# The first block's down projection by pairs of weight panels, seven block products for eight, on one Trainium2 core

## What is computed

```python
h = jnp.square(jax.nn.relu(jnp.einsum("bsd,df->bsf", x, w_ff1[l])))
ff = jnp.einsum("bsf,fd->bsd", h, w_ff2[l])
x = layer_norm(DEEPNORM_ALPHA * x + ff, ln2_g[l], ln2_b[l])
```

## Time and profile before

| | us |
|---|---|
| median of the runs (1448.5 to 1450.94) | 1448.59 |
| profiled execution: span from first to last instruction | 1446.2 |
| what lies around the span, by the median | 2.4 |
| feed-forward part of the first block (64 panels), matmuls | 348.4 |
| TensorE busy | 1419.5 |
| VectorE busy | 820.0 |
| ScalarE busy | 612.0 |
| GpSimd busy | 134.1 |

### The profile page before, as it was taken

How to read it: one execution, slowest core, us unless ns; L and a number is a source line. 1 busy time by engine, 2 the same in 40 slices (tenths; PEclk the granted TensorE clock), 3 DMA queues, 4 the chain that set the end, 5 groups by cost and what they waited for, 6 DMA issues and landing times.

```text
span 1446.2 us, 20161 instructions
## 1 busy us (share of the span) xinstructions
PE 1419.5 (98%) x7966; PEld 1137.2 (79%) x7966; DVE 820.0 (57%) x1408; ACT 612.0 (42%) x1113; POOL 134.1 (9%) x119
## 2 busy tenths in 40 slices
PE   8999999999999999999999999999999999999998
PEld 6777677788878888888877777786778888888887
DVE  4645555557574343443468776676565763664464
ACT  4644455543363242322336755345444431442334
POOL 0000000002200000000012010350020110110012
PEclk9999999999999999999999999999999999999999
DMA  7222221113223222222223212110232322223212
GB/s 254 73 83 92 80 89 64 68 58 117 102 62 114 96 93 103 93 103 96 93 100 133 95 65 74 59 47 1 96 109 73 116 102 96 94 102 102 84 66 70
DMA packets 41501, 130.94 MB, mean 91 GB/s; under 512 B 4928, under 2 KB 7360, under 8 KB 41408
## 3 DMA queue, kind: packets, MB, share of 16 engines
q1 hardware_dynamic: 40544, 128.60, 25.4%
q10 hardware_dynamic: 864, 1.05, 0.2%
HBM read 124.92 MB, written 4.19 MB: 89 GB/s over the span
## 4 chain that ended last, share of the span: by engine, by line
PE 88%; DVE 5%; ACT 3%; issue 2%; DMA 1%; POOL 0%; SPq 0%; POOLq 0%; DVEq 0%; ACTq 0%
PE bank L1300 85%; PE bank L1303 3%; ACT Fm L1697 2%; DVE Fm L2160 1%; DVE Wlo L2055 1%; DVE Fm L2055 1%; ACT Whi L1697 1%; DVE Fm L2063 1%; DMA Fm<-in_relb_dram 1%; SPq L2756 0%; POOL Fm L2659 0%; DVE Xf L2055 0%; DMA Fm<-in_x_dram 0%; DVE sm L2059 0%; DVE Fm L2059 0%
## 5 line engine op out<-in xcount | busy, mean ns | idle before, releaser
L1300 PE MATMUL bank<-Rm,Whi 128*128 128x512 f32 (+1 forms) x2840 | 874.8, 389 | 9.2 <-ACT Whi L1697 6.0
L1300 PEld LDWEIGHTS bank<-Rm,Whi 128*128 128x128 f32 x2840 | 533.0, 188 | 119.9 <-ACT Whi L1697 6.0
L1300 PE MATMUL bank<-Rm,Wlo 128*128 128x512 f32 (+1 forms) x1420 | 565.6, 398 | 1.1 <-issue 0.9
L2055 DVE TENSOR_TENSOR Wlo<-Wraw,Whi 128x1024 fp32r<-128x1024 f32 (+2 forms) x225 | 284.2, 1267 | 141.6 <-ACT Whi L1697 141.0
L1300 PEld LDWEIGHTS bank<-Rm,Wlo 128*128 128x128 f32 x1420 | 267.7, 189 | 61.7 <-issue 7.6
L1697 ACT ACTIVATE Whi<-Wraw 128x1024 fp32r<-128x1024 f32 (+2 forms) x225 | 232.5, 1038 | 191.8 <-PE bank L1300 186.2
L1300 PE MATMUL bank<-Xr,Whi 128*128 128x512 f32 (+1 forms) x760 | 228.5, 382 | 0.0
L2659 POOL TENSOR_TENSOR Fm<-Fm 128x512 f32<-128x512 f32 (+1 forms) x89 | 112.3, 1269 | 773.5 <-ACT Fm L1697 480.3
L1300 PEld LDWEIGHTS bank<-Xr,Whi 128*128 128x128 f32 x760 | 141.1, 188 | 27.9
L1697 ACT ACTIVATE Fm<-bank 128x512 f32<-128x512 f32 (+4 forms) x200 | 92.3, 482 | 147.8 <-PE bank L1300 103.2
L2055 DVE TENSOR_TENSOR Fm<-Fm,bank 128x512 f32<-128x512 f32 (+2 forms) x130 | 77.8, 622 | 120.7 <-PE bank L1300 120.2
(11 more groups left out here) (100 smaller groups left out, 712.7 us busy)
## 6 DMA issues: line engine op xcount, KB each, us to landing
Wraw<-in_w_in_dram SPq DMA_DIRECT2D x67, 512.0 KB, 3.2
Wraw<-in_w_ff_dram SPq DMA_DIRECT2D x64, 512.0 KB, 3.2
Wraw<-in_w_up_dram SPq DMA_DIRECT2D x44, 512.0 KB, 3.2
Wraw<-in_w_o_dram SPq DMA_DIRECT2D x16, 512.0 KB, 3.2
Wraw<-in_w_down_dram SPq DMA_DIRECT2D x16, 512.0 KB, 3.1
Wraw<-in_w_ab_dram SPq DMA_DIRECT2D x8, 512.0 KB, 3.2
Wraw<-in_w_down_end_dram SPq DMA_DIRECT2D x8, 384.0 KB, 2.8
Fm<-in_relb_dram SPq DMA_DIRECT2D x8, 256.0 KB, 4.1
```

The costliest lines, as they stand in the source:

```text
L1300: return e.matmul(o, l, r, start=first, stop=last)
L2055: return e.tensor_tensor(o, x, y, op)
```

## The change

Down panels are taken in pairs (two output tiles, n and n+1). Over the 8 hidden tiles of a group, the pair is a product of 2 x 2 blocks: the two output tiles and the two halves of the contraction (4 row tiles each) on the weight side, and tokens 0 to 255 (`EARLIER`) and 256 to 511 (`LATER`) on the other. It is now made by seven products of blocks instead of eight, after Winograd: each product is 4 steps of three matmuls of 256 columns. The order of rows in `w_ff2` is changed on the host so that the halves are even and odd hidden tiles.

- Weights: of a pair's four half panels a11, a12, a21, a22 GpSimd makes s1 = a21 + a22, s2 = s1 - a11, s4 = a12 - s2, s3 = a11 - a21 (128 x 512 each) from the raw panels. They are split in two *parts* of 1024 elements (s1 and s2; s4 and s3) by ScalarE (`blocksplit`) and VectorE (`blocklow`). Of the second panel only the half a22 is split as before; the first is split whole. The buffers of the sums and of their parts are single.
- Hidden tiles: after each second up panel, `hidden` makes three sums on GpSimd (one of 512 elements, two of 256) and the high and low parts of 256 + 3 x 512 elements in place of 2 x 512.
- Outputs: the products land in three banks (`total`, `single`, `fifth`), and VectorE adds them to the output tiles in six `fold`s: 256 elements four times, 512 twice. Product 6 is added on product 1 in its bank, 3 on 5, 7 on 6; so product 6 waits for fold 1, 3 for fold 5, 7 for fold 6.
- ALPHA is multiplied in by ScalarE after up panels 0 to 7 of the first group.
- The P ring has 6 banks. Loads wait for the sums of the pair 4 panels before, too, and the constants' load for the last hidden tiles.
- In the last group both `sum` items come after the pair.

```diff
+PRODUCTS = (1, 2, 5, 6, 4, 3, 7)
...
         while st["splits"] < min(len(PANELS), upto) and st["splits"] - HL < st["done"]:
...
+            n = st["splits"]
+            do("split", n)
             st["splits"] += 1
+            if pair_of(n) == n - 1:
+                do("blocks", n - 1)
+                st["sums"] += 1
...
+    def sum_parts(upto):
+        while st["parts"] < upto and st["parts"] // 2 < st["sums"]:
+            do("blocksplit", PAIRS[st["parts"] // 2], st["parts"] % 2)
+            do("blocklow", PAIRS[st["parts"] // 2], st["parts"] % 2)
+            st["parts"] += 1
...
             if p == LOW_AT:
                 low_weights()
+                sum_parts(2 * st["pairs"] + 2)
...
+    def seven_products(name, i):
+
+        n = take(name, i)
+        take(name, i + 1)
+        r = st["pairs"]
+        for bank in ("total", "single", "fifth"):
+            do(bank, n)
+        sum_parts(2 * r + 1)
+        do("product", n, 1)
+        sum_parts(2 * r + 2)
+        low_weights(st["taken"] + 1)
+        do("fold", n, 1)
+        do("product", n, 2)
+        low_weights()
+        do("product", n, 5)
+        do("fold", n, 5)
+        do("product", n, 6)
+        do("fold", n, 6)
+        sum_parts(2 * r + 3)
+        do("product", n, 4)
+        do("fold", n, 4)
+        do("product", n, 3)
+        do("fold", n, 3)
+        do("product", n, 7)
+        do("fold", n, 7)
+        st["pairs"] += 1
+        st["done"] = n + 2
...
+    do("ring", "P", (3, 7, 1, 2, 4, 0))
     for kind, i in FF1:
         if kind == "up":
             n = first[i] if i < 3 else project("w_ff1", i)
             do("relu2", i)
+            if i % 2:
+                do("hidden", i // 2)
+            if i < 8:
+                do("alpha", i)
         else:
-            for m in range(8):
-                n = project("w_ff2", 8 * i + m)
-                do("down", n)
+            for m in range(0, 8, 2):
+                seven_products("w_ff2", 8 * i + m)
                 if i == 3:
                     do("sum", 1, m)
+                    do("sum", 1, m + 1)
...
+                elif what == "product":
+                    n, p = i
...
+                    if p in (1, 2, 5):
+                        bank_free({1: "total", 2: "single", 5: "fifth"}[p], n)
+                    else:
+                        if p != 4:
+                            w.wait_ge(SG["fold"], fold_end(n, {6: 1, 3: 5, 7: 6}[p]))
...
+                    for k in range(4):
+                        q = 4 * g + k
+                        w.wait_ge(SG["hid_hi"], moving_made(q, p))
+                        w.wait_ge(SG["hid_lo"], moving_made(q, p))
+                        xh, xl = moving(q, p)
+                        s = slice(128 * k, 128 * k + 128)
+                        add(o, lo[:, s], xh, p in (1, 2, 5) and k == 0)
+                        add(o, hi[:, s], xl)
+                        m = add(o, hi[:, s], xh, False, k == 3)
+                    m.then_inc(SG["product"], 1)
...
+                elif what == "blocksplit":
+                    n, half_ = i
+                    r = PAIR_NO[n]
+                    w.wait_ge(SG["blocks"], 4 * r + 2 * half_ + 2)
+                    if r > 0:
+                        w.wait_ge(SG["product"], product_end(PAIRS[r - 1], 7 if half_ else 6))
+                    hi, _, raw = combined(half_)
+                    act(hi, raw).then_inc(SG["block_hi"], 1)
...
+                elif what == "hidden":
+                    q, = i
+                    f, b = F(SQUARE + 2 * q % 4), F(SQUARE + 2 * q % 4 + 1)
+                    for n, of in ((3, f[:, EARLIER]), (0, b), (1, F(SUMS)), (2, F(SUMS + 1))):
+                        if n in (0, 3):
+                            w.wait_ge(SG["squared"], 2 * q + (1 if n == 3 else 2))
+                        else:
+                            w.wait_ge(SG["hid_sums"], 3 * q + (1 if n == 1 else 3))
...
+                        act(hidden_part(q, n)[0], of).then_inc(SG["hid_hi"], 1)
...
+                elif what == "blocks":
...
+                    w.wait_ge(*loaded(n))
+                    w.wait_ge(*loaded(n + 1))
+                    if r > 0:
+                        w.wait_ge(SG["block_lo"], 2 * r - 1)
+                    tt(s1, a21, a22, ALU.add).then_inc(SG["blocks"], 1)
+                    w.wait_ge(SG["blocks"], 4 * r + 1)
+                    tt(s2, s1, a11, ALU.subtract).then_inc(SG["blocks"], 1)
+                    w.wait_ge(SG["blocks"], 4 * r + 2)
+                    if r > 0:
+                        w.wait_ge(SG["block_lo"], 2 * r)
+                    tt(s4, a12, s2, ALU.subtract).then_inc(SG["blocks"], 1)
+                    tt(s3, a11, a21, ALU.subtract).then_inc(SG["blocks"], 1)
...
                     if n >= RAW:
                         w.wait_ge(SG["w_hi"], n - RAW + 1)
                         w.wait_ge(*low_part(n - RAW))
+                        if pair_of(n - RAW) is not None:
+                            w.wait_ge(SG["blocks"], 4 * PAIR_NO[pair_of(n - RAW)] + 4)
```

More of the change, by code:

```diff
@@ L119, with pair_of, product_end @@
 NTH = {p: n for n, p in enumerate(PANELS)}
+DOUBLE = ("w_ff2",)
+PAIRS = [n for n, (name, i) in enumerate(PANELS) if name in DOUBLE and i % 2 == 0]
+PAIR_NO = {n: r for r, n in enumerate(PAIRS)}
+def pair_of(n):
+    name, i = PANELS[n]
+    return n - i % 2 if name in DOUBLE else None
+PRODUCTS = (1, 2, 5, 6, 4, 3, 7)
+def product_end(n, p):
+    return 7 * PAIR_NO[n] + PRODUCTS.index(p) + 1
 RAW = 4
@@ L145, in order_of_work @@
     work, side, later = [], [], []
-    st = {"loads": 0, "splits": 0, "lows": 0, "taken": 0, "done": 0}
+    st = {"loads": 0, "splits": 0, "lows": 0, "taken": 0, "done": 0, "sums": 0, "parts": 0, "pairs": 0}
     def do(*item):
@@ L907, in sb @@
             return ctx.enter_context(nc.sbuf_tensor(name, shape, dt))
+        with nc.sbuf_tensor("Er", [128, 49, 512], F32R) as Er:
+            pass
         Fm = sb("Fm", [128, 49, 512])
@@ L1078, in low_part, with finished @@
             return SG["w_lo"], at("low", n)
+        def finished(n):
+            if pair_of(n) is not None:
+                return SG["product"], product_end(pair_of(n), 2 if pair_of(n) == n else 4)
+            return SG["panel"], n + 1 - sum(2 for m in PAIRS if m < n)
         def emptied(n):
@@ L1236, in summed @@
             if tag == 1:
-                return SG["down"], at("down", NTH["w_ff2", 24 + j])
+                return SG["fold"], fold_end(NTH["w_ff2", 24 + j - j % 2], 7 if j % 2 else 3)
             if tag == 2:
@@ L1300, in mm, with add @@
                 return e.matmul(o, l, r, start=first, stop=last)
+            def add(o, l, r, first=False, last=False):
+                return e.matmul(o, l, r, start=first, stop=last, skip_group_check=True)
             def tr(o, x):
@@ L1699, in panel @@
             def panel(n):
-                w.wait_ge(SG["panel"], n + 1)
+                w.wait_ge(*finished(n))
                 return bank("panel", n)
@@ new lines, in vector_engine @@
+                    tt(F(SQUARE + j % 4), F(RELU + j % 3), F(RELU + j % 3), ALU.mult).then_inc(SG["squared"], 1)
+                elif what == "hidden":
+                    q, = i
+                    f, b = F(SQUARE + 2 * q % 4), F(SQUARE + 2 * q % 4 + 1)
+                    for m, (n, of) in enumerate(((3, f[:, EARLIER]), (0, b), (1, F(SUMS)), (2, F(SUMS + 1)))):
+                        w.wait_ge(SG["hid_hi"], 4 * q + m + 1)
+                        hi, lo = hidden_part(q, n)
+                        tt(lo, of, hi.bitcast(F32), ALU.subtract).then_inc(SG["hid_lo"], 1)
+                elif what == "fold":
+                    n, p = i
+                    m = PANELS[n][1] % 8
+                    w.wait_ge(SG["product"], product_end(n, p))
+                    w.wait_ge(SG["alpha"], m + 2)
+                    if p == 1:
+                        x, b = F(m)[:, EARLIER], bank("total", n)[:, EARLIER]
+                    elif p == 5:
+                        x, b = F(m + 1)[:, LATER], bank("fifth", n)[:, EARLIER]
+                    elif p == 6:
+                        x, b = F(m)[:, LATER], bank("total", n)[:, EARLIER]
+                    elif p == 4:
+                        w.wait_ge(SG["fold"], fold_end(n, 1))
+                        x, b = Fm[:, m:m + 2, EARLIER], bank("single", n).rearrange("p (n c) -> p n c", n=2)
+                    elif p == 3:
+                        w.wait_ge(SG["fold"], fold_end(n, 6))
+                        x, b = F(m)[:, LATER], bank("fifth", n)[:, EARLIER]
+                    else:
+                        w.wait_ge(SG["fold"], fold_end(n, 4))
+                        x = F(m + 1).rearrange("p (n c) -> p n c", n=2)
+                        b = bank("total", n)[:, EARLIER].unsqueeze(1).broadcast_to([128, 2, 256])
+                    if PAIR_NO[n] >= 4:
+                        w.wait_ge(SG["fold"], fold_end(PAIRS[PAIR_NO[n] - 4], 7))
+                    tt(x, x, b, ALU.add).then_inc(SG["fold"], 1)
```

131 lines of the change are left out of this document (92 added, 39 removed).

## The result

The changed kernel takes **1498.42 us** (median of 4 runs, 1497.92 to 1502.28) against 1448.55 for the kernel before in the same session (1447.34 to 1450.94): ratio 1.0346, 95% interval [1.0332, 1.0361]. It is slower, as forecast, but by 49.9 us in place of 20.7, outside the range and above every rival's time. Span 1496.9 us.

What follows compares the result with a forecast made beforehand. TensorE's matmuls were taken to bound the feed-forward stage, other engines' work hidden. Terms -12.8 + 0.4 + 10.4 + 14.4 + 7.8 + 0.5 = +20.7 us gave 1469.3 us; range 1448 to 1478.

Steps and rivals of the forecast that it cites:

- every rival's time: Whole kernel: no lock 1448 to 1456 (0.18); matmuls decide 1436 to 1445 (0.11); last two about 1479, 1483 (0.11 together).
- Term 1: Down-panel pairs: 84 matmuls of 256 columns replace 48 of 512, gaining 0.80 us a pair, -12.8 us over 16 pairs.
- Term 2: Nine undisturbed pairs, second to fourth of the first three groups: fold 1 just in time for product 6; +0.4 us.
- GpSimd taking the lock in every pair: Rival on the undisturbed pairs: GpSimd gets in first, their cost becomes 10 us, about 1479; 0.11 together with another rival.
- the lock: GpSimd additions and VectorE instructions with both inputs in SBUF exclude each other, 1.15 us per GpSimd addition of 512.
- Term 3: Last group's pairs 2 to 4: product 6 waits for fold 1, with layer-norm sums behind each pair; +10.4 us (8.4 to 12).
- Term 4: First pair of each of the first three groups: fold 1 late for product 6, 4.8 us each, +14.4 us.
- at nothing: Items priced at no cost: ALPHA scalings on ScalarE, 32 old adds falling off, loads, product boundaries.
- Term 5: Last group's first pair, no up panel before it: products 1 and 6 wait; +7.8 us (3.7 to 8.2).
- the no-lock case: Rival: collisions cost 0.25 us and no more, only queue order delays the last group; 1448 to 1456 us, chance 0.18.
- Term 6: The tail: both adds of the last two tiles come behind fold 7; +0.5 us.
- If the stage is shorter than 345 us, the prediction is wrong in its queues: Sign for the first block's feed-forward stage, 401.6 to 750: under 345 us the queues were misjudged, not the matmuls.

Runs made afterwards that it cites:

- Run 3: Changed kernel with GpSimd's four sums of weight blocks made for one column of 512 only, output not the reference's: 1469.93 us, ratio 1.0148.
- Run 5: Changed kernel with the third next-projection panel's split and low part moved ahead of the last pair's product 3: 1491.53 us, ratio 1.0293.
- run 7: Changed kernel with third panel's split earlier, folds 1 and 5 ahead of low parts, last group's layer-norm sums moved into the next pair: 1478.5 us, ratio 1.0201.
- run 6: Changed kernel with filler matmuls of constants on an unused bank, their number fitted to TensorE's waits: 1489.89 us, ratio 1.0285.
- run 4: Changed kernel with 8, 9 or 6 filler matmuls of constants on an unused bank where TensorE waits: 1499.79 us, ratio 1.0353.

## Why the prediction was right or wrong

- **Term 1, right.** Pairs without a wait take 84 x 0.120 us at clock 1.00; -12.8 us stands.
- **Term 2, right within 0.4 us.** None of the nine undisturbed pairs waits. The case of GpSimd taking the lock in every pair is out.
- **Term 3, right.** Waits 3.39 + 3.82 + 2.70 = 9.9 us, said 10.4. (Its own parts, 3.9 to 4.1 twice and 2.9, give 10.7 to 11.1.) Run 3 shows 7.2 of them without the lock, a little under the lower bound of 8.4.
- **Term 4, place right, size low by 3.** Product 6 waits 4.38, 4.66 and 4.67 us, said 4.8 each. The first group's product 1 also waits, 2.81, and a panel 0.56 earlier: 17.1 in place of 14.4. That pair's hidden sums aren't in this wait: PE goes on 0.14 us behind a low part of the squared tile itself (VectorE, 453.06 to 453.47), and the sums begin only at 453.21. What is late in the first group is ScalarE. It takes the relu of up panel 5 straight behind other work; in the second group, for up panel 13 in the same place, it stands idle until TensorE's last matmul:

```profile
437.10 0.58 ACT L1850 ACTIVATE Fm<-bank 128x512 f32<-128x512 f32 x1
...
528.54 0.60 ACT L1850 ACTIVATE Fm<-bank 128x512 f32<-128x512 f32 x1 [2.73 <-PE bank L1421]
```

  In the 37.4 us before 437.0 it is busy for 26.1 us, in the 37.5 before 528.5 for 13.6. The layer norm's items and the scalings by ALPHA stand there only in the first group. The prediction put the scalings at nothing; which of the two makes ScalarE late was not tried.
- **Term 5, high by 2.** 5.24 + 0.60 = 5.8 us, said 7.8.
- **The idle time as a whole** is therefore 32.8 us, where terms 2 to 5 said 33.0. That they agree to 0.2 is luck: term 4 is low by 2.7 and terms 2, 3 and 5 are high by 0.4, 0.5 and 2.0. The schedule built from the prices of the kernel before held to some 3 us a term, and the lock with it: the no-lock case (1448 to 1456) is refuted by run 3, which changes the additions' length alone and takes the 512-element low part from 1524 to 685 ns. What run 3 doesn't part is the blocking from the additions' own length in the chain; the durations of VectorE's instructions show the one, not the split of the 28.5 us between them.
- **The step that failed: a microsecond of wait was priced at one microsecond.** Each term took the matmuls behind a wait to run at 0.120 us. They ran at 0.213 until the clock rose again: 32.8 us of waiting cost 17.2 us more in longer matmuls, 15.0 of them by the two spacings. The prediction read clock 1.00 with PE busy for 348.38 of 348.40 us, and kept the clock when it gave up the second. No wait in that stage of the kernel before could have warned it, but that kernel's start could. Its first matmuls, behind 5.99 us of idle time, and those a few us on:

```profile
5.99 0.80 PE L1300 MATMUL bank<-Rm,Whi 128*128 128x512 f32 x1 [5.99 <-ACT Whi L1697]
...
9.10 0.63 PE L1300 MATMUL bank<-Rm,Wlo 128*128 128x512 f32 x1
...
10.38 0.63 PE L1300 MATMUL bank<-Rm,Wlo 128*128 128x512 f32 x1
...
15.53 0.39 PE L1300 MATMUL bank<-Rm,Wlo 128*128 128x512 f32 x1
...
16.21 0.39 PE L1300 MATMUL bank<-Rm,Wlo 128*128 128x512 f32 x1
```

  Three matmuls of 512 columns take 1.28 us at first and 0.68 later, 0.427 against 0.227 each. This trace has no clock record ahead of 12.6 us, but in the changed kernel matmuls of 512 columns are 0.42 to 0.43 us apart where the clock is 0.50 (at 809 us, in the window 798.75 to 812.40). So that matmuls behind idle time can be slower, and by how much, was there to read. The Trainium skill (TensorE: Matmul & The Clock Gate, "HAM oscillation — how this bites in real kernels") describes such a loss behind waits and counts it as the time at the lower level times one half. By that figure 37.5 us at 1.2 GHz would cost an estimated 19 us. The rows say 15 to 17: TensorE stands idle in 4.2 of the 37.5 us, and a 256-column matmul grows by 1.78 times and not by 2.
- **Term 6 and "at nothing", the second step that failed, by 15.** The tail was priced at 0.5 us, and 15.4 were measured behind the stage. 1.64 of it is a wait at the norm's start, where the kernel before had none. And nothing was said of the panels that TensorE works on *during* the norm. Taking two panels at once, with `done` set only after both, lets one split fewer run ahead, and the third panel's split falls behind the norm's affines: 10.68 us of wait, then matmuls at 1.2 GHz. In the change's terms: `st["splits"] - HL < st["done"]` was read for the pairs and not for the stage behind them. Run 5 gives 6.9 back; in run 7 what follows the stage is five shorter still (699.5 us).
- **The miss as a whole:** by spans +50.7 in place of +20.7. Of the 30.0 between them 17.1 stand in the stage and 14.9 behind it, less the 2.0 by which the stage began earlier.
- **"If the stage is shorter than 345 us, the prediction is wrong in its queues":** it was 385.65. The signs named (256-column matmuls 0.12 apart, waits behind folds, low parts over 1.23 us, other pairs near 10.1) all appeared; the sign that would have caught the failure, the clock's row, was not among them.

## What to carry to other kernels

The clock of 1.00 in a stretch where TensorE never pauses says nothing of the clock once it does. When a change takes work off TensorE and puts new waits in its place, price the waits with the slower matmuls behind them: here another half of the idle time on top. GpSimd is no free engine beside a VectorE that reads two SBUF operands: 113 us of GpSimd additions and 80 VectorE additions weighed about the same on VectorE (269.9 and 272.6 us busy), and the second has no chain across engines. And where a unit of work is doubled (two panels at once), follow every lookahead counted in those units into the next stage.

## What the runs showed of the hardware that was not expected

- After waits of 2.70 us and more in the stage the granted clock was at 1.2 GHz for a stretch (windows at 0.77 over 10 us); after those of 0.56 and 0.60 it was not (at 732.78 six matmuls took 0.98 us, not 1.65). Matmuls of 256 columns are 0.213 us apart there, 0.120 at 2.4 GHz.
- Useless matmuls in the waits made the kernel 8.5 us faster (run 6), and none faster where they overran the waits by 2 us (run 4).
- GpSimd's 256-element additions of the hidden tiles took 1067 ns each (32 of them, none over 1077), though 32 others in the second layer of the same execution average 857, half of them under 740. So it isn't the size alone; what it is wasn't tried. The two groups, first in the stage, then behind it:

```profile
L2858 POOL TENSOR_TENSOR Fm<-Fm 128x256 f32<-128x256 f32 x32 | 34.1, 1067 | 2.5
...
L2858 POOL TENSOR_TENSOR Fm<-Fm 128x256 f32<-128x256 f32 x32 | 26.7, 857 | 102.4 <-DVE Fm L2230 89.2 <-ACT Fm L1850 13.0
```
